# Zero products ahead of the first rows, split value products without zero banks, and two GLU operands moved into the attention's last pair

## The reference, cut to what matters

```
h = rms_norm(x);  xa, u, q, k, v, gates = split(h @ w_in)
ya = rglru_branch(xa)
z  = gelu(S5(u));  gl = z @ glu_w + glu_b          # 512 -> 1024
yb = gl[:, :512] * sigmoid(gl[:, 512:])
yc = dilated_window_attention(q, k, v)              # scores, softmax, p @ v
merged = sum_i sigmoid(gate_i) * (branch_i @ w_proj_i)
x += rms_norm(merged @ w_out);  x += rms_norm(relu(rms_norm(x) @ w1)^2 @ w2)
```

## Time and profile before

| what | value |
|---|---|
| median of 3 runs | 1919.81 us (1918.68 to 1920.53) |
| the profiled execution | 1915.44 us, its span 1913.7 us |
| PE busy, PEld busy | 1867.9 us (98%), 1773.7 us (93%) |
| DVE, ACT, POOL busy | 1214.1 us (63%), 707.0 us (37%), 670.4 us (35%) |
| granted clock, mean | 0.996 |
| prompt's attention | 748 to 870 us, some 20.6 us for a pair |
| GLU products (L2958) | from 870.4 us |

### The profile page before, as it was taken

The page is one execution under the profiler, slowest core; times in us unless marked ns, Lnnn a source line. Parts: engine busy times, 40 slices in busy tenths (PEclk is TensorE's granted clock), DMA queues, the critical chain, the costliest instruction groups (busy, mean ns, idle before and its releaser), DMA issues.

```text
span 1913.7 us, 35874 instructions
## 1 busy us (share of the span) xinstructions
PE 1867.9 (98%) x15182; PEld 1773.7 (93%) x15182; DVE 1214.1 (63%) x1509; ACT 707.0 (37%) x942; POOL 670.4 (35%) x342
## 2 busy tenths in 40 slices
PE   8999999999999999999999999899999999999997
PEld 8999999989989897668999999889999999999996
DVE  8899652255444546663445736885655675878988
ACT  6412212253443445663200134423444445433332
POOL 0022111212111123442466641227677761532514
PEclk9999999999999999999999999999999999999998
DMA  5422433866675753632344332433433457565333
GB/s 178 112 97 76 135 109 113 249 205 204 215 231 189 232 179 118 188 113 101 125 179 154 125 119 80 154 121 106 152 135 135 170 199 273 181 213 190 116 136 137
DMA packets 191415, 298.73 MB, mean 156 GB/s; under 512 B 37248, under 2 KB 133248, under 8 KB 187680
## 3 DMA queue, kind: packets, MB, share of 16 engines
q1 hardware_dynamic: 184352, 270.60, 43.7%
q10 hardware_dynamic: 6912, 25.96, 3.4%
HBM read 215.12 MB, written 79.28 MB: 154 GB/s over the span
## 4 chain that ended last, share of the span: by engine, by line
PE 81%; DVE 10%; issue 3%; ACT 2%; DMA 2%; POOL 2%; SPq 0%; POOLq 0%; DVEq 0%; ACTq 0%
PE ps L2619 37%; PE ps L3131 25%; PE ps L2994 3%; PE ps L2958 2%; PE ps L2878 2%; PE ps L2848 1%; PE ps L2791 1%; PE ps L2887 1%; PE ps L2634 1%; PE ps L2772 1%; PE ps L2920 1%; DMA w_raw<-in_w 1%; DVE stage L2321 1%; DVE xq L2389 1%; PE ps L2753 1%
## 5 line engine op out<-in xcount | busy, mean ns | idle before, releaser
L1154 POOL TENSOR_TENSOR w_lo<-w_raw,w_hi 128x1024 fp32r<-128x1024 f32 x48 | 122.1, 2544 | 622.6 <-ACT w_hi L1303 622.6
L2619 PE MATMUL ps<-op_hi,w_hi 128*128 128x352 f32 x1392 | 309.0, 330 | 0.1
L2619 PE MATMUL ps<-op_lo,w_hi 128*128 128x352 f32 x1392 | 301.7, 325 | 0.0
L2619 PE MATMUL ps<-op_hi,w_lo 128*128 128x352 f32 x1392 | 300.2, 323 | 0.0
L2619 PEld LDWEIGHTS ps<-op_hi,w_hi 128*128 128x128 f32 x1392 | 233.5, 188 | 15.2 <-issue 13.2
L2619 PEld LDWEIGHTS ps<-op_lo,w_hi 128*128 128x128 f32 x1392 | 237.6, 188 | 0.0
L2619 PEld LDWEIGHTS ps<-op_hi,w_lo 128*128 128x128 f32 x1392 | 236.7, 188 | 0.0
L1377 ACT ACTIVATE stage<-ps 128x1056 f32<-128x1056 f32 x48 | 50.5, 1052 | 280.8 <-PE ps L2619 280.8
L1161 POOL TENSOR_TENSOR w_hi<-w_raw,zeros 128x1024 fp32r<-128x1024 f32 x26 | 64.2, 2470 | 174.8 <-DMA w_raw<-in_w 73.9
L3131 PE MATMUL ps<-do_hi,w_hi 128*128 128x264 f32 x560 | 114.0, 285 | 1.7 <-DVE w_lo L2445 1.0
L3131 PE MATMUL ps<-do_lo,w_hi 128*128 128x264 f32 x560 | 113.2, 284 | 0.0
(11 more groups left out here) (467 smaller groups left out, 4618.8 us busy)
## 6 DMA issues: line engine op xcount, KB each, us to landing
w_raw<-in_w SPq DMA_DIRECT2D x101, 512.0 KB, 4.3
t_raw<-tmp_h SPq DMA_DIRECT2D x28, 1056.0 KB, 5.7
kc<-in_k_cache SPq DMA_DIRECT2D x48, 448.0 KB, 5.5
vc<-in_v_cache SPq DMA_DIRECT2D x48, 448.0 KB, 6.3
out_keep<-stage ACTq DMA_DIRECT2D x24, 528.0 KB, 2.7
tmp_gate_d<-stage ACTq DMA_DIRECT2D x24, 528.0 KB, 4.6
gate_t<-tmp_gate_d SPq DMA_DIRECT2D x24, 528.0 KB, 3.6
tmp_h<-o_t SPq DMA_DIRECT2D x18, 528.0 KB, 3.1
```

The costliest lines, as they stand in the source:

```text
L1154: pool.tensor_tensor(lo, w_raw[:, b], hi.bitcast(F32), ALU.subtract).then_inc(w_split[b], 1)
L2619: mm = pe.matmul(ps[:, 3 * dst + q, 0:BLK], w[:, b, w0 + n], x[:, k, q * BLK:(q + 1) * BLK], start=(n == 0 and part == 0), stop=(n == len( ...
```

## The change

Four edits. (1) `first_pair` waits for `w_zero` and does `WARM` = 14 products of `zeros` with 512 columns into bank 5, whose content is not read, before its first block. (2) The 12 products of zeros in `at_near` go; the first value product into a bank carries `start=True` in their place, and each product of 256 columns is done as two of 128, the later query block first. (3) ACT makes `gop_hi[0]` after its copy of step 37 and `gop_hi[1]` after its copy of step 38, and 2 and 3 after that of step 41 as before; DVE makes `gop_lo[0]` at the end of iteration 39 and `gop_lo[1]` at the end of iteration 40. (4) PE does the products of blocks 0 and 1 for the first GLU output tile (18 matmuls of 352 columns) before the outputs of step 41; the rest follows as before.

```diff
--- before.py
+++ after.py
@@ -75,6 +75,7 @@
 E_ALL = E_DOWN + 2 * NP * len(SUPER)
 SPARE = E_ALL - 1
 HALF, QUART = N // 2, N // 4
+WARM = 14
 LAST_P, LAST_B = 4, N // 4
 LAST_BANKS = 4
 LAST_COLS = [(1, 0), (1, 1), (0, 0), (0, 1)]
@@ -1497,9 +1498,11 @@
                 at_copy(g)
                 if g % PER == V_STEP and g // PER + 1 < HP:
                     at_values(g // PER + 1)
-                if g >= NG - 2:
-                    for k in range(2):
-                        glu_high(2 * (g - NG + 2) + k)
+                if g in (NG - 5, NG - 4):
+                    glu_high(g - NG + 5)
+                if g == NG - 1:
+                    for k in range(2, K_B):
+                        glu_high(k)
 
 
             act.wait_ge(op_l, K_B)
@@ -2193,9 +2196,8 @@
                     at_outputs(g // PER, 7)
                 if g % PER == 0 and g:
                     at_outputs(g // PER - 1, 6)
-                if g >= NG - 1:
-                    glu_low(0)
-                    glu_low(1)
+                if g in (NG - 3, NG - 2):
+                    glu_low(g - NG + 3)
             at_outputs(HP - 1, 6)
             for k in range(2, K_B):
                 glu_low(k)
@@ -2637,6 +2639,9 @@
 
             def first_pair():
 
+                te.wait_ge(w_zero, 1)
+                for n in range(WARM):
+                    pe.matmul(ps[:, 5, :], zeros[:, 0:P].bitcast(F32R), zeros[:].bitcast(F32R), start=True, stop=True)
                 for k in range(KD - 2):
                     te.wait_ge(n_in.lo, k + 1)
                     for b in range(2):
@@ -2885,7 +2890,7 @@
                     at_block = [8 * max(x - 1, 0) + 4 * a + b for x, b in uses]
                     got = pt_blocks[:, at_block[0]:at_block[-1] + 1:at_block[-1] - at_block[0] if n > 1 else 1]
                     mm = pe.matmul(ps[rows, 6 + q // 4, P * (q % 4):P * (q % 4 + n)].rearrange("p (q n) -> p q n", q=n),
-                                   vn[:, w % 2, j, rows], got, start=False, stop=(j == 1))
+                                   vn[:, w % 2, j, rows], got, start=(j in (7, 3) and q == j), stop=(j == 1 and q == j))
                 return mm
 
             def at_near(g):
@@ -2897,15 +2902,14 @@
                     te.wait_ge(sa_o, ROUNDS)
                 if w and s in (0, 4):
                     te.wait_ge(at_o, 2 * w - 1 + (s == 4))
-                if s in (0, 4):
-                    pe.matmul(ps[:, 7 - s // 4, :], zeros[:, 0:P].bitcast(F32R), zeros[:].bitcast(F32R), start=True, stop=False)
                 for j in STEP_TILES[s]:
                     uses = [(j, 2 if j == 1 else j > 0)]
                     if j % 4 != 3:
                         uses.append((j + 1, int(j == 0)))
                     if j == 4:
                         near_block(w, 3, [(4, 0)])
-                    mm = near_block(w, j, uses)
+                    for use in reversed(uses):
+                        mm = near_block(w, j, [use])
                 return mm
 
             def at_far(g):
@@ -2933,31 +2937,39 @@
             at_values(0)
             for g in range(2, AHEAD):
                 at_scores(g)
+            def glu_part(m, dst, ks):
+                for k in ks:
+                    te.wait_ge(op_l, k + 1)
+                    for part, (w, x) in enumerate(((w_hi, gop_hi), (w_hi, gop_lo), (w_lo, gop_hi))):
+                        for q in range(NBLK):
+                            mm = pe.matmul(ps[:, 3 * dst + q, 0:BLK], w[:, m % 2, K_B * dst + k], x[k][:, piece(q)],
+                                           start=(k == 0 and part == 0), stop=(k == K_B - 1 and part == 2))
+                if k == K_B - 1:
+                    mm.then_inc(mm_ready[dst], 1)
+
             for g in range(NG + 1):
                 if g + AHEAD < NG:
                     at_scores(g + AHEAD)
                 if g < NG:
                     at_transposes(g)
+                if g == NG:
+                    te.wait_ge(at_max, 2 * MEMBERS[NG])
+                    te.wait_ge(w_split[0], P_GLU + 1)
+                    te.wait_ge(mm_free[0], USES[P_GLU])
+                    glu_part(0, 0, range(2))
                 if g:
                     at_outputs(g - 1)
                 if g % PER == V_STEP and g // PER + 1 < HP:
                     at_values(g // PER + 1)
 
-            te.wait_ge(at_max, 2 * MEMBERS[NG])
             te.wait_ge(at_even, copied(P_GRAN[NG - 1][0]))
             te.wait_ge(at_odd, copied(P_GRAN[NG - 1][1]))
-
+            glu_part(0, 0, range(2, K_B))
             for m in range(K_B):
-                for dst in range(2):
+                for dst in range(m == 0, 2):
                     te.wait_ge(w_split[m % 2], P_GLU + m // 2 + 1)
                     te.wait_ge(mm_free[dst], USES[P_GLU] + m)
-                    for k in range(K_B):
-                        te.wait_ge(op_l, k + 1)
-                        for part, (w, x) in enumerate(((w_hi, gop_hi), (w_hi, gop_lo), (w_lo, gop_hi))):
-                            for q in range(NBLK):
-                                mm = pe.matmul(ps[:, 3 * dst + q, 0:BLK], w[:, m % 2, K_B * dst + k], x[k][:, q * BLK:(q + 1) * BLK],
-                                               start=(k == 0 and part == 0), stop=(k == K_B - 1 and part == 2))
-                    mm.then_inc(mm_ready[dst], 1)
+                    glu_part(m, dst, range(K_B))
 
             for m in range(KD // 2):
                 for dst in range(2):
```

## The result

| | before | after |
|---|---|---|
| median (range, runs) | 1919.38 us (1914.54 to 1923.07, 14) | 1925.76 us (1922.32 to 1929.51, 14) |
| the profiled execution, its span | 1915.44, 1913.7 us | 1922.32, 1920.5 us |
| granted clock, mean | 0.996 | 0.993 |

The changed kernel takes 1.0035 times as long [1.0026, 1.0044]: 6.7 us more [5.0, 8.4], where 1.8 us more was forecast. The medians differ by 6.4 us and the profiled executions by 6.8 to 6.9. In the page of after the chain still runs over PE, with 80% of it where it was 81%.

The account below looks back on a forecast made before the run. PE bounds the kernel, with 81% of the chain; the last steps hang on ACT's and DVE's order. Terms -0.2 - 2.3 + 0.1 + 4.2 = +1.8 us gave a median of 1921.6 us, range 1916.8 to 1925.3.

Parts of the forecast that it names:

- the clock behind the new pauses: Rival: clock falls in the last steps' new pause (+0.9 to +1.7 us) or at the start (+1.6); chance 0.19.
- Start, -0.20: First rows: zeros raise the clock early, but block 1 waits for DVE's low part, so only 0.20 us is saved.
- Zero banks and split, -2.3 and +0.1: Attention: ten of 12 removed zero products save 0.23 us each, -2.3; splitting 36 double products costs +0.1 us.
- rival C: Attention: the split costs, up to +5.4 us (1927 us); over 0.2% slower from 0.27 us a four; chance 0.08.
- Last steps, +4.2 by order: Last attention steps into the GLU: early operands delay PE, so block 3 starts at 880.95, not 876.74, +4.2 us.
- the three waits: Last steps: PE waits some 2 us for ACT's copy, some 2 for DVE's copy, 3 for `gop_lo` behind outputs(41).
- This is the costly edit: Last steps: DVE's `glu_low(0)` ahead of copy(40) delays that copy to 869.6, so PE idles some 2 us.
- work moved, not added: Last steps: PE's 18 early GLU products take 2.9 us ahead of outputs(41), counted as moved.
- A pause of 4.62 us was followed by the granted clock 0.50, the one of 1.92 us by none: Clock rival's evidence from before's profile: the long pause brought the clock down, the last steps' 1.92 us one did not.
- the new 3.2 us pause: Last steps: PE stands still from 875.4 to 878.7, behind outputs(41), before block 2 of the GLU.
- an offset: Whole kernel: the median shown is 4.4 us above the profiled execution, so 1917.2 us becomes a 1921.6 us median.
- the shift was taken as constant: From GLU block 3 on: streams before and after are equal, so a shift of its start shifts the end.

Follow-up runs that it names:

- the filled kernel: The changed kernel plus 29 products of zeros where PE waits, nothing else moved; 1919.76 us, 1.0012 against the kernel before.
- part 3 alone: The kernel before with only edits (3) and (4), early GLU operands and 18 early products; 1926.27 us, 1.0044 against the kernel before.

## Why the prediction was wrong

The sum had four terms, and all four held within some tenths of a microsecond. What failed is a fifth that it put at nothing: the clock behind the new pauses, kept as a rival, belonged in the sum.

- **Start, -0.20.** Right: -0.24 at block 1, and the new wait of 1.19 us for DVE. Timed alone it is within its interval of nothing.
- **Zero banks and split, -2.3 and +0.1.** Right by time (-1.9 us [-3.8, -0.2]) and somewhat high by the pairs: 20.30 us where 20.2 was forecast. It is not the split, which costs 0.03 us a pair. The two removed zeros are worth 0.33 us a pair in the stream and not 2 x 0.23; the stretch where one goes is shorter by 0.23, and some 0.14 us comes back behind it, in small steps at the transposes of `qkv` and the scores. Which engine or queue gives these steps was not settled. The limit of rival C was read too high: against four doubles at their stream's 0.43 us, as in the term itself, 0.24 us for each single four gives the +3.8, not 0.27, and fours at their stand-alone 0.37 give +11, not +5.4. It decides nothing, since the split costs 0.2 us.
- **Last steps, +4.2 by order.** Right: the three waits came in their places within 0.2 us, and with the clock held the order costs +4.5. But the price doesn't lie where the text put it. "This is the costly edit" was said of DVE's `glu_low(0)` ahead of copy(40), and "work moved, not added" of PE's 18 products. DVE's edit does cost (0.06% with ACT's edit, 0.23% with both), but with it one step later block 3 comes only 0.2 to 0.9 us earlier than in the filled kernel, and PE's 18 products cost as much or more (0.23% without them, 0.44% with them, 3.2 us in the two traces): they hold back the outputs, and so the last `yo` and `gop_lo[2]`, as the sum itself counts.
- **The clock: the step that failed.** The prediction put it as "A pause of 4.62 us was followed by the granted clock 0.50, the one of 1.92 us by none", looked in the last steps at the new 3.2 us pause alone, and gave the rival 0.19 and at most +1.7 us. The change makes three pauses, of 2.16, 2.00 and 3.19 us, and each was followed by 0.50 in some execution: the first in three kernels with ACT's edit (and not in after and the one with DVE's part a step later), the second in after's profile, the third in all three that have it. It cost some 2 us in after's profile, 4.4 us by the ratios against the filled kernel, and more where it fell early, since the last steps at half speed stay on the path. The row that the rule rested on was one draw: with the zeros at the start alone the same 1.92 us pause was followed by a fall. Before's 77 runs beside the experiments had mean clocks of 0.992 to 0.996, and the profiled execution stands at the top of these. That its time was 4.4 us under the median was in the prediction, but only as an offset, and not as a sign that the clock falls more often than that profile shows.
- Behind the first GLU tile the shift was taken as constant. It is +7.4 at 891.74 and +6.8 at the end of the span.

The times add up from parts: order +4.5 (the filled kernel's profile), attention -1.9 and start -0.2, clock +4.4 by the filled kernel: +6.8 against 6.7 measured. They are not independent (the filled kernel holds all parts), so this is a check of consistency and not a proof of each size.

The Trainium skill (TensorE: Matmul & The Clock Gate, HAM oscillation — how this bites in real kernels) warns of idle stretches between bursts of matmuls. The runs agree and go further: the clock fell behind pauses down to 1.92 us, shorter than the page has them, and not in every execution. Here the measurement decides.

Not tried: the zero products removed with the 256-column products kept. In the changed kernel only the first product into a bank carries `start=True`, and the first products of its other query blocks don't, so whether a 256-column product without the flag would have served, and the split could be spared, is open. Nor was PE's own edit run without the other two.

## What to carry to other kernels

Work moved ahead costs whatever is queued behind it on its own engine: put it in a slot where that engine stands idle in the profile (with PE's order the same, the same two GLU operands cost 0.23% in one order of ACT and DVE and brought 0.14% in another). Work that only changes places on TensorE costs too if what it now stands in front of releases another engine that TensorE will wait for. Reckon with each pause of TensorE of about 2 us and more that is added twice: as a pause, and as products at half speed behind it in some of the executions. A clock that held in one profiled execution is no rule; read the mean clock of all runs, and test with products of zeros in the pauses.

## What the runs showed of the hardware

- The granted clock went to 0.50 behind five of ten pauses of PE of 1.92 to 2.17 us in the last attention steps of the profiled kernels (1.92, 2.00, 2.15 and twice 2.17 us), and not behind the other five (twice 1.92, 2.00 and twice 2.16 us). Behind the one of 3.19 us it did in all three. What decides it was not found.
- A stretch at 0.50 in small transposes and value products lasted 17 us in two kernels though PE was busy 4.00 of 4.00 us in windows of it; in a third (ACT's edit alone) it was over after some 3.5 us of the same work. Behind the long ones the GLU's products were back at 1.00 (0.99 in 881 to 887 with part 3 alone).
- Products of zeros raise the clock as others do, by the pace: behind 14 of them, from 1.32 us on, the first real products took 0.20 and then 0.163 us each in place of 0.35 and 0.293. The granted clock of the profile reads 1.00 throughout these first microseconds, at both paces.
- Two products of 128 columns in place of one of 256 cost 36 x about 0.005 us: nothing that a run can tell.
